# Mamba-2 scan in a hybrid decoder layer: the new state's products and their addition moved ahead of the output's

## What is computed

```python
scores = jnp.einsum('nclhd,ncshd->nclsh', Cc, Bc) * decay
y_diag = jnp.einsum('nclsh,ncshp->nclhp', scores, xc)
to_end = jnp.exp(acum[:, :, -1:, :] - acum)
states = jnp.einsum('nclhd,nclhp->nchpd', Bc * to_end[..., None], xc)
def step(h, inp):
    dec, st = inp
    return h * dec[..., None, None] + st, h
y_off = jnp.einsum('nclhd,nchpd->nclhp', Cc * jnp.exp(acum)[..., None], h_prev)
y = (y_diag + y_off)          # then y + d_skip * x, * silu(z), and an RMS norm
```

## Time and profile before

| | us |
|---|---|
| median of 3 runs (2566.48 to 2568.35) | 2567.28 |
| the profiled execution | 2565.84 |
| its span | 2563.6 |
| PE busy in it | 2423.4 |
| DVE busy in it | 1232.8 |
| ACT busy in it | 846.6 |
| POOL busy in it | 277.0 |

### The profile page before, as it was taken

How to read it: one execution, slowest core, us unless ns; L and a number is a source line. 1 busy time by engine, 2 the same in 40 slices (tenths; PEclk the granted TensorE clock), 3 DMA queues, 4 the chain that set the end, 5 groups by cost and what they waited for, 6 DMA issues and landing times.

```text
span 2563.6 us, 43225 instructions
## 1 busy us (share of the span) xinstructions
PE 2423.4 (95%) x17509; PEld 1422.6 (55%) x17509; DVE 1232.8 (48%) x2843; ACT 846.6 (33%) x1533; POOL 277.0 (11%) x305
## 2 busy tenths in 40 slices
PE   7899979999888999999989999999999999999999
PEld 3455536555444655544455554445655447788887
DVE  3445545566646766742544554235566521412222
ACT  4443234465434543431433231124332111301210
POOL 0111222011101211000111100011101001000000
PEclk8999988999999999999999999999999999999999
DMA  6444364555584567775444555533454543222222
GB/s 212 171 162 165 110 219 140 193 202 179 175 257 156 202 199 239 247 245 195 146 134 137 163 166 172 167 111 115 156 167 160 166 161 122 95 91 99 91 99 81
DMA packets 327588, 414.44 MB, mean 162 GB/s; under 512 B 62111, under 2 KB 248095, under 8 KB 327136
## 3 DMA queue, kind: packets, MB, share of 16 engines
q1 hardware_dynamic: 327392, 411.69, 48.9%
HBM read 300.00 MB, written 111.62 MB: 161 GB/s over the span
## 4 chain that ended last, share of the span: by engine, by line
PE 75%; DVE 6%; ACT 3%; issue 2%; DMA 1%; SPq 1%; POOL 0%; DVEq 0%; ACTq 0%; POOLq 0%
PE core_dense L2299 64%; PE core_spare L2399 2%; PE core_spare L2413 1%; PE core_spare L2387 1%; PE core_spare L2425 1%; PE core_spare L2548 1%; DVE core_col L2013 1%; DVE core_p L1939 1%; ACT core_p L1715 1%; PE core_spare L2542 1%; PE core_spare L2528 0%; PE core_spare L2482 0%; PE core_spare L2534 0%; DVE core_h L1907 0%; PE core_spare L2529 0%
## 5 line engine op out<-in xcount | busy, mean ns | idle before, releaser
L2299 PE MATMUL core_dense<-core_u,core_ring 128*128 128x512 f16 (+2 forms) x4800 | 871.3, 342 | 20.9 <-ACT core_yt L1688 5.7
L2299 PEld LDWEIGHTS core_dense<-core_u,core_ring 128*128 128x128 f16 x4800 | 469.7, 99 | 395.8 <-issue 41.0
L2299 PE MATMUL core_dense<-core_r_hi,core_ring 128*128 128x512 f16 (+2 forms) x2560 | 649.0, 339 | 2.7 <-DVE core_h L1907 1.5
L2299 PE MATMUL core_dense<-core_r_lo,core_ring 128*128 128x512 f16 (+2 forms) x1280 | 434.0, 339 | 0.0
L2299 PEld LDWEIGHTS core_dense<-core_r_hi,core_ring 128*128 128x128 f16 x2560 | 250.4, 98 | 197.6 <-issue 5.5
L2299 PE MATMUL core_dense<-tok_u,core_ring 128*128 128x512 f16 x1152 | 267.1, 388 | 17.6 <-DMA core_ring<-scratch_kept_w 17.6
L1680 ACT ACTIVATE core_r<-core_dense 128x512 f32<-128x512 f32 (+2 forms) x160 | 82.5, 516 | 529.0 <-PE core_dense L2299 529.0
L1895 DVE TENSOR_TENSOR core_r<-core_r 128x512 f32<-128x512 f32 (+2 forms) x160 | 96.9, 606 | 321.5 <-ACT core_r L1680 321.1
L628 PE MATMUL tok_prod<-tok_w_hi,tok_u 128*128 128x512 f16 (+1 forms) x768 | 200.5, 351 | 0.0
L2299 PEld LDWEIGHTS core_dense<-tok_u,core_ring 128*128 128x128 f16 x1152 | 114.2, 100 | 148.8 <-issue 14.9
L2299 PEld LDWEIGHTS core_dense<-core_r_lo,core_ring 128*128 128x128 f16 x1280 | 125.2, 98 | 93.4 <-issue 0.7
(11 more groups left out here) (309 smaller groups left out, 2733.1 us busy)
## 6 DMA issues: line engine op xcount, KB each, us to landing
core_ring<-scratch_kept_w SPq DMA_DIRECT2D x264, 512.0 KB, 4.3
scratch_kept_w<-core_ring SPq DMA_DIRECT2D x72, 512.0 KB, 5.6
core_qkv<-out_tok SPq DMA_DIRECT2D x48, 384.0 KB, 5.7
core_staged<-in_w_up SPq DMA_DIRECT2D x32, 512.0 KB, 4.7
core_staged<-in_w_down SPq DMA_DIRECT2D x32, 512.0 KB, 4.7
out_tok<-tok_tok SPq DMA_DIRECT2D x16, 644.0 KB, 3.0
core_piece<-in_c_kt SPq DMA_DIRECT2D x32, 288.0 KB, 3.8
core_piece<-in_c_v SPq DMA_DIRECT2D x16, 576.0 KB, 4.3
```

Source lines behind the costliest of these rows:

```text
L2299: ins = pe.matmul(bank, w[:, k, part, :], s, start=first and j == 0, stop=last and j == 2, skip_group_check=True)
```

## The change

In `scan_2` of PE the two matmuls of the new state, with their waits, go ahead of the wait for `mix_ready` and of the 16 matmuls of the output. In `scan_2` of DVE the addition to the state, with its waits, goes ahead of the wait for `yy_done` and the skip. Nothing else is touched; ACT, POOL and SP have the same instructions in the same order. The first piece of the diff is DVE's, the second PE's.

```diff
                 def scan_2(c):
+                    dve.wait_ge(faded, c + 1)
+                    dve.wait_ge(h_done, c + 1)
+                    dve.tensor_tensor(state[:, 1 - c % 2, :], state[:, 1 - c % 2, :], spare[0][:, :], ALU.add).then_inc(state_ready, 1)
                     dve.wait_ge(yy_done, c + 1)
                     for kk in range(4):
                         last = dve.scalar_tensor_tensor(y[:, kk, :], xbc[:, c % 2, kk, :], d_skip[:, kk:kk + 1], spare[5][:, kk * P:(kk + 1) * P],
                                                        ALU.mult, ALU.add)
                     last.then_inc(skipped, 1)
-                    dve.wait_ge(faded, c + 1)
-                    dve.wait_ge(h_done, c + 1)
-                    dve.tensor_tensor(state[:, 1 - c % 2, :], state[:, 1 - c % 2, :], spare[0][:, :], ALU.add).then_inc(state_ready, 1)
...
                 def scan_2(c):
                     pe.wait_ge(x_ready, c + 1)
+                    pe.wait_ge(b_ready, c + 1)
+                    free(pe, "H", c)
+                    for gr in range(2):
+                        last = pe.matmul(spare[0][:, gr * 256:(gr + 1) * 256], b_tok[:, gr, :], xte[:, gr * 256:(gr + 1) * 256], start=True, stop=True)
+                    last.then_inc(h_done, 1)
                     pe.wait_ge(mix_ready, c + 1)
...
                     last.then_inc(yy_done, 1)
-                    pe.wait_ge(b_ready, c + 1)
-                    free(pe, "H", c)
-                    for gr in range(2):
-                        last = pe.matmul(spare[0][:, gr * 256:(gr + 1) * 256], b_tok[:, gr, :], xte[:, gr * 256:(gr + 1) * 256], start=True, stop=True)
-                    last.then_inc(h_done, 1)
```

## The result

Ten runs of each kernel give 2577.09 us median (2572.19 to 2581.73) with the change and 2568.66 (2566.48 to 2573.92) before it. The ratio is 1.0031 with a 95% interval of 1.0020 to 1.0043: slower by 8.0 us (0.31%, the interval is 5.1 to 11.0 us; 8.4 by the medians), where +4.8 was forecast. The measured time is outside the forecast's range (2568.8 to 2574.6). 1.4 us of the miss is the median of before itself, which was 2567.28 in the three runs shown; the rest is the change.

What follows compares the result with a forecast made beforehand. PE was taken as the bound, busy 2423.4 of 2563.6 us. Six longer waits (+4.9) and chunks 0 to 3 (-0.15) gave +4.8 us on the median 2567.28: 2572.1 us, range 2568.8 to 2574.6.

Steps and rivals of the forecast that it cites:

- The six waits: PE's waits for the skip behind scan_2 in chunks 8 and 11 to 15 grow, costing 4.9 us in all.
- The cost of the moved products: State's products in their new place on PE take 0.86 to 0.97 us, taken as 0.92.
- The drain rule: Tiling-mode changes drain PE's array; the moved state's products pay no drain, favouring 0.86 us and a sum of 4.4.
- the sum: Whole kernel: 4.9 us from the six waits less 0.15 from chunks 0 to 3, +4.8 us.
- the long idle of chunk 3: PE's wait ahead of chunk 3's sums of squares, 2.81 us before, grows to some 4.2 us.
- The first rival: Clock fall in chunk 3 becomes certain or longer: +1.8 us at most, 6.6 in all, 2573.9 us; chance 22%.
- Chunks 0 to 3: Gaps before the scores get filled, but the chain to the sums of squares limits the gain: -0.15 us in all.
- The dense chunks: Chunks 4 to 7, 9 and 10, with a dense unit behind scan_2: only slack shrinks, cost nothing.
- The second and third rivals: Second: filled gaps in chunks 0 to 3 carry through, +0.4 us, 13%; third: six waits also don't grow, -4.5, 7%.

Runs made afterwards that it cites:

- fill: Changed kernel plus the state's products repeated into an unread bank behind the output's in the six chunks; 2573.48 us against 2567.78 before, ratio 1.0023; again 2576.93, ratio 1.0028.
- dve_only: Kernel before with DVE's part alone: addition ahead of the skip, PE in the old order; 2590.24 us against 2569.08, ratio 1.0081.
- pe_only: Kernel before with PE's part alone: state's products ahead of the output's in all 16 chunks, DVE in the old order; 2574.49 us against 2569.08, ratio 1.0025.
- ten_only: Kernel before with the new order only in the ten chunks without a sampled unit behind scan_2; 2566.93 us against 2567.78, ratio 0.9998.
- bank3_after: Changed kernel with the six sampled units behind scan_2 writing bank spare[3] instead of spare[5]; 2564.39 us against 2567.78 before, ratio 0.9995.
- the second of the changed kernel: The changed kernel run and profiled once more, nothing further altered, beside the filled one; 2577.14 us against 2568.93 before, ratio 1.0036.

## Why the prediction was wrong, point by point

**The six waits: right.** Forecast 1.2 to 1.4 us each and some 7.5 in all; measured 1.31 and 7.8. The cost of the moved products was bounded at 0.86 to 0.97 us and taken at 0.92; it is 0.86, so the term is 6 x 0.86 - 0.57 = 4.6 in place of 4.9. The drain rule of the Trainium skill ("TensorEngine Tiling (Array Packing)", Key Properties), which spoke for the lower bound, agrees with this trace: behind a full-width matmul the state's products pay nothing extra, and the change from width 128 to 64 costs 0.31 in place of 0.22 whoever stands ahead of it.

**What is missing from the sum: the clock behind these waits.** This is the step that failed. The prediction weighed the clock at one place only, the long idle of chunk 3, and noted that 2.75 and 2.81 us had led to a fall and 1.21 had not. From this it took, without saying so, that a wait of 1.3 us is safe, and put the clock's price behind the six waits at nothing. One of three is not safe: 8 falls in 24, 1.7 us each, which is 2 x 1.7 = 3.4 us in a profile on average. With 4.6 that is 8.0, the measured difference. That it fits to a tenth is luck, as the interval is 5.1 to 11.0 us and the medians of the filled kernel don't show the clock's share by themselves. Behind the 1.98 us of dve_only the fall came every time. Right behind the wait stand the short matmuls of the sampled unit, 27 in 0.85 us in chunks 12 to 15 and 66 in 0.99 us in chunks 8 and 11, which the trace counts as busy; what part they have in the falls wasn't tried.

The trace of before had a warning, in the attentions at 1757 us: two waits shorter than the 2.75 and 2.81 us that the prediction counted, 0.6 us of small matmuls between them, and behind them 1.2 GHz (0.50 of full speed from 1761 to 1763 us). All thirteen profiles have this fall.

```profile
1758.90 0.63 PE L2596 MATMUL core_spare<-core_ident,core_soft 128*128 128x128 f32 x4 [1.66 <-DVE core_o L1939]
...
1760.87 0.61 PE L2599 MATMUL core_spare<-core_ident,core_soft 128*32 128x128 f32 x2 [1.33 <-DVE core_qk_t L1964]
```

The Trainium skill, "TensorE: Matmul & The Clock Gate", Part 1, says that the gate goes by how busy TensorE has been lately; that a longer wait brings more falls, and a filled one none, agrees with it. The first rival had the right mechanism, and its +6.6 lies in the measured interval, but it put the falls at the wrong place.

**Chunks 0 to 3: right in kind.** The filled gaps were not to be gains, because the chain through skip, gate and square ends last. The measured waits for the scores are 1.85, 0, 0 and 0.30 us and those for the squares 1.96, 0.52, 0.52 and 4.39; the four chunks together gave 0.0 where -0.15 was forecast. Here is chunk 0, against the earlier trace rows:

```profile
615.40 0.45 PE L2533 MATMUL core_spare<-core_dec,core_xdt 128*64 128x128 f32 x4 [1.85 <-DVE core_dec L2087]
...
618.30 0.69 DVE L2098 TENSOR_TENSOR core_state<-core_state,core_spare 128x512 f32<-128x512 f32 x1
618.90 1.12 DVE L2101 SCALAR_TENSOR_TENSOR core_y<-core_xbc,core_d_skip,core_spare 128x128 f32<-128x128 f32 x4
...
621.39 0.63 ACT L1769 ACTIVATE core_m<-core_y 128x512 f32<-128x512 f32 x1 [6.29 <-POOL core_y L1584]
622.07 1.16 PE L2542 MATMUL core_spare<-core_m,core_ones 128*128 128x128 f32 x8 [1.96 <-ACT core_m L1769]
```

The addition waits out the convolution and then holds up the skip by 0.6, as the prediction had it, and pe_only shows the same 0.6 twice. And chunk 3, against the earlier trace rows: the wait of 2.81 us has become 4.39.

```profile
684.46 1.51 PE L2542 MATMUL core_spare<-core_m,core_ones 128*128 128x128 f32 x8 [4.39 <-ACT core_m L1769]
```

Not foreseen: in four of the nine profiles with PE's new order in these chunks (ten_only, bank3_after, fill, the second of the changed kernel) the stretch to G3 was 72.1 us, not 70.4 or 69.2. A fall of the clock had come some 9 us after the scores of chunk 0, behind its two waits of nearly 2 us, and had cost 1.7.

**The dense chunks: nearly right.** "Nothing" was 0.1 us each in favour: from chunk 5's output products to chunk 6's there are 25.63 us in place of 25.72.

**The first rival** put the whole of its extra loss at chunk 3, behind G3, as a fall that is certain or lasts longer. All four profiles in which chunk 3's wait is 4.39 us have a fall there, but so have the three with 2.81, so it cost nothing new in the first. In one thing the rival was right: in ten_only and bank3_after the clock stayed low for some 7 us (689.5 to 696.5 and 685.5 to 692.5), twice as long as before and in the changed kernel, and the sums of squares with the 48 dense matmuls behind them took 13.7 and 13.9 us for 13.2 from start to end. That is 0.5 to 0.7 us in two profiles, not 1.8.

**The second and third rivals**, gains of some 4.5 us carried through, are refuted by ten_only: its interval reaches 3.1 us below before, and its ratio is 0.9998. The third also needed the six waits to stay as they were, and they are 1.31 us each.

## What to carry to other kernels

Before an instruction is moved ahead, look for who waits directly behind its old place: on a bound engine a free filler under a wait is worth its whole length, and moving it only turns it into idle time. Price each new wait of TensorE by the clock too, as a chance times the cost of a fall, and look in the whole trace whether a fall that was avoided at one place stands at another. And an earlier result is no gain if the wait that it removes is followed by another that hangs on the same chain; here the better change was to take away what makes the sampled units wait, another bank, though only together with PE's new order, and in one of two sets of rounds, did that come out ahead of the kernel before.

## What the runs showed of the hardware

Behind `scan_2` of the six chunks, with the short matmuls of a sampled unit (0.85 or 0.99 us) between the wait and the dense work, TensorE fell to 1.2 GHz after an idle of 1.31 us in 8 of 24 cases, after 1.98 us in 6 of 6, after 0.45 us or less in 0 of 48. Behind an idle of 1.89 us directly ahead of dense work it fell in 6 of 13 profiles. A fall costs 1.7 us of dense work. Where it comes can differ in two runs of one kernel (chunks 8 and 14 in one, 8, 12 and 13 in the other). And the time up to the scores of chunk 0, in which nothing was changed, is between 613.0 and 620.8 us in the thirteen profiles, a difference as large as the one that was studied; only stretches behind it can be compared with each other to a tenth of a microsecond.
